# Stick-breaking attention: its cumulative sums in two fp32r passes, and its head pairs started beside other projections

## The chip, the cores and the metric

The kernel runs on one core of a Trainium2 chip. The metric is the device time of one execution in microseconds. The kernel before took 1529.96 us (median of three runs, 1529.09 to 1530.27).

## The reference, cut to what matters

Two network blocks of two layers each work on 256 tokens of width 1024. The change touches one mixer only, the stick-breaking attention of the second block's first layer:

```python
q, k, v = jnp.split(x @ w_in, 3, axis=-1)            # 16 heads of 64
for blk in range(S // Q_BLOCK):                      # two query blocks of 128
    z = einsum('bqhd,bkhd->bhqk', q[:, t0:L], k[:, :L]) * scale
    past = s_idx < t_idx
    log_fail = where(past, log_sigmoid(-z), 0.0)
    later = lax.cumsum(log_fail, axis=3, reverse=True) - log_fail
    a = where(past, exp(log_sigmoid(z) + later), 0.0)
    outs.append(einsum('bhqk,bkhd->bqhd', a, v[:, :L]))
return concatenate(outs) @ w_out
```

## The kernel before, in words

All matrix products with weights are done in three fp32r passes: a weight unit (128 x 1024 floats, 512 KB) is loaded by the SyncE queue into `w_raw`, ScalarE copies it to fp32r (`w_high`, L1493), VectorE subtracts (`w_low`, L1943), and TensorE multiplies high by high, high by low and low by high (L1092 to L1105). A planner (`Plan`) writes one list of steps, and every engine works through its own part of that list strictly in that order. Splits run five units ahead of the products (`prefetch`), and the split of a unit waits for the product of six units before it.

For the stick-breaking mixer (`stick_breaking`, L561) the input matrix of 3072 columns is cut into six panels of 512 columns and four units each: two of queries, two of keys (`sb_in`, features on the partitions, 24 products of 256 columns per unit), two of values (`sb_values`, tokens on the partitions, 12 products of 512 columns per unit). The 16 heads are worked on as 8 pairs. Keys stand on the partitions and queries along the row, so a head has a 128 x 384 tile: 256 queries against the first 128 keys, and the last 128 queries against the last 128 keys. A pair has 768 columns. Its steps:

- `sb_a`: TensorE makes the logits z in fp32 (L1317, L1319) in PSUM; ScalarE takes abs, exp and ln (L1717, L1719, L1721).
- `sb_b`: VectorE makes the fail term (L2278) and multiplies it by a mask of -1 and 0 over all 768 columns (L2280).
- `sb_c`: TensorE adds the sums over later keys onto z (L1332): per head, products of 256, 128 and 128 columns in fp32 with a triangular and an all-ones tile. VectorE clips and masks (L2287), ScalarE takes exp, the weights (L1728).
- `sb_d`: TensorE multiplies the weights by the values (L1345, L1347); ScalarE copies the high part (L1476), VectorE makes the low part (L1904) for the output product `sb_out`.

In iteration n of the loop stand `sb_d(n-3)`, `sb_c(n-2)`, `sb_b(n-1)`, then one or two weight units, then `sb_a(n)`. The units are the eight of `sb_values` (two in iterations 0 and 1, one in 2 to 5) and then four of `sb_out` (iterations 6 to 9). The copy of a finished value panel out of PSUM by ScalarE is `take_v` (L1704), the scaling of query and key panels by VectorE `take_qk` (L2266). The logits of even and odd pairs have slots 0 and 1 of PSUM (two banks each), the outputs of pairs banks 6 and 7 (slot 3). Panel 0 of `sb_out` gathers in slot 2, panel 1 in slot 1. After the loop the last four units of `sb_out` are done for the first 128 tokens and then for the others.

Of the kernel before, what the change touches and what calls it, by code (L numbers as in the profile page):

```python
# [14 lines left out]
P = 128  # L15
# [41 lines left out]
def weight_plan():  # L57
# [97 lines left out]
for _name, _w in (("ident", P), ("not_below", P), ("ones", P), ("cos_m", TT * ROPE // 2),  # L155
                  ("sin_m", TT * ROPE // 2), ("cos_g", TT * HD // 2), ("sin_g", TT * HD // 2),
                  ("inv_freq", DIL_ROT // 2), ("pool_edge", POOL_G * 2 * POOL_PAD), ("sb_neg", 3 * P),
                  ("sb_add", 3 * P), ("dil_add", 9 * P)):
    CONSTS[_name] = (_n, _n + _w)
    _n += _w  # L160
N_CONSTS = _n
N_HELD = CONSTS["sb_neg"][0]


def constants():
# [21 lines left out]
    past = np.concatenate([i[:, None] < np.arange(SEQ)[None, :], i[:, None] < i[None, :]], 1)  # L187
    put("sb_neg", np.where(past, -1.0, 0.0))
    put("sb_add", np.where(past, 0.0, MASKED))
# [18 lines left out]
def slot_of(name, layer, panel):  # L208
# [8 lines left out]
         "branch_gqa": (1, 0), "branch_pool": (2, 3), "branch_mla": (0, 1), "out": (0, 1),  # L217
         "ffn_up": (2, 1, 3, 2, 0, 1, 3, 2, 0, 1, 3, 2), "ffn_down": (0, 1), "sb_in": (0, 1, 2), "sb_values": (2,), "sb_out": (2, 1),
         "dil_qk": (1, 2, 0), "dil_values": (2,), "dil_out": (0, 2)}
# [6 lines left out]

BY_FEATURE = ("gates_early", "gates", "branch_gqa", "branch_pool", "branch_mla", "ffn_up", "sb_in", "ff_in")

# [18 lines left out]
class Plan:  # L247
# [313 lines left out]
    def stick_breaking(self):  # L561
        add, g, n_pairs = self.add, STAGE_SB, SB_H // 2
        add("load_sb")
        self.after(4, lambda: (add("diag", g), add("row", g)))
        self.whole("sb_in", 0, lambda panel: add("take_qk", panel))
        values = self.linear("sb_values", 0, lambda panel: add("take_v", panel))
        product = self.linear("sb_out", 0, None, SKEWED)
        add("sb_table")
        for n in range(n_pairs + 3):
# [14 lines left out]
        for _ in product:  # L584
            pass
# [130 lines left out]
class Kernel:  # L716
# [109 lines left out]
    def stick_memory(self):  # L826
        with ExitStack() as ctx:
# [4 lines left out]
            self.sb_masks = sb("sb_masks", 2 * NZ)  # L832
            part = lambda ap: ap.rearrange("p (j n) -> p j n", j=2)
            self.sb_weights = [part(sb(f"sb_weights{i}", 2 * NZ)) for i in range(2)]
            parts = [part(self.scr[:, i * 2 * NZ:(i + 1) * 2 * NZ]) for i in range(5)]
# [57 lines left out]
    def sync(self, eng):  # L893
# [5 lines left out]
        for step in self.plan.steps:  # L899
# [32 lines left out]
            elif kind == "load_sb":  # L932
                eng.dma_start(self.rows, dram["second_rows"][0, 0].partition_broadcast(P)
                              ).then_inc(sem("gains_loaded"), 16)
                at = CONSTS["sb_neg"][0]
                eng.dma_start(self.sb_masks, dram["consts"][:, at:at + 2 * NZ]).then_inc(sem("sb_masks_loaded"), 16)
# [29 lines left out]
    def operands(self, u):  # L966
# [18 lines left out]
        if name == "ffn_down":  # L985
            return self.ffn[l]
        if name in ("sb_in", "sb_values"):
            return self.features[STAGE_SB]
# [14 lines left out]
    def operand_ready(self, q, u, k, t):  # L1003
# [14 lines left out]
        elif name == "ffn_down":  # L1018
            q.wait_ge(sem("ffn_low"), at("ffn_split", l, k // 4))
        elif name in ("sb_in", "sb_values"):  # L1020
            q.wait_ge(sem("features_low"), at("turn", STAGE_SB, k // 2))
# [15 lines left out]
    def tensor(self, eng):  # L1037
        q = Queue(eng, None)
        sem, at, bank = self.sem, self.at, self.bank
        ident, ones, not_below = self.const("ident"), self.const("ones"), self.const("not_below")  # L1040

# [23 lines left out]
        for step in self.plan.steps:  # L1065
# [243 lines left out]
            elif kind == "sb_a":  # L1309
                j, = key  # L1310
                b = j % 2
                z = self.slot[b].rearrange("p (j n) -> p j n", j=2)
                q.wait_ge(sem("qk_taken"), at("take_qk", 3))
                acquire(2 * b, 2 * b + 1)
# [8 lines left out]
            elif kind == "sb_c":  # L1323
                j, = key
                b, fail = j % 2, self.sb_fail[j % 2]
# [113 lines left out]
    def taken_panel(self, step):  # L1439
# [10 lines left out]
        if kind == "take_qk":  # L1450
            return "sb_in", key[0]
        if kind == "take_v":
            return "sb_values", key[0]
        if kind == "take_dv":
# [8 lines left out]
    def scalar(self, eng):  # L1463
# [19 lines left out]
        for step in self.plan.steps:  # L1483
# [215 lines left out]
            elif kind == "take_v":  # L1699
                panel, = key  # L1700
                self.panel_done(q, "sb_values", 0, panel)
                a = by_token(self.acc("sb_values", panel))
                for t in range(TT):
# [3 lines left out]
            elif kind == "sb_table":  # L1707
                eng.preload_act_table_set("natural_log_exp_and_others")

            elif kind == "sb_a":  # L1710
# [9 lines left out]
                q.settle()  # L1720
                act(soft, soft, ACT.Ln, bias=1.0).then_inc(sem("soft_ready"), 1)  # L1721

            elif kind == "sb_c":
# [168 lines left out]
    def vector(self, eng):  # L1892
# [42 lines left out]
        for step in self.plan.steps:  # L1935
# [325 lines left out]
            elif kind == "take_qk":  # L2261
                panel, = key
                part = slice(4 * (panel % 2), 4 * (panel % 2) + 4)
                self.panel_done(q, "sb_in", 0, panel)
                q.wait_ge(sem("row_ready"), at("row", STAGE_SB))
                stt((self.sb_q if panel < 2 else self.sb_k)[:, part, :], by_tile(self.acc("sb_in", panel)),  # L2266
                    HD ** -0.5 if panel < 2 else 1.0, self.row(4), ALU.mult, ALU.mult).then_inc(sem("qk_taken"), 1)

            elif kind == "sb_b":
                j, = key  # L2270
                zs = self.slot[j % 2].rearrange("p (j n) -> p j n", j=2)[:, :, 0:NZ]
                neg = self.sb_masks[:, 0:NZ].rearrange("p (o n) -> p o n", o=1).to_broadcast([P, 2, NZ])
                fail = self.sb_fail[j % 2]
                q.wait_ge(sem("soft_ready"), at("sb_a", j))
                q.wait_ge(sem("sb_masks_loaded"), 16)
# [394 lines left out]
```

## Time and profile before

| what | us |
|---|---|
| median of three runs | 1529.96 |
| the profiled execution, its own time | 1527.88 |
| its span, first to last instruction | 1526.1 |
| TensorE busy in the span | 1493.5 |
| VectorE busy | 1045.5 |
| ScalarE busy | 839.8 |
| first logits of the mixer start | 870.98 |
| first pass of `sb_out` over the first tokens starts | 929.02 |

The span is told from the first to the last instruction; the profiled execution's own time is 1.8 us longer. A busy share is a mean over the whole span. In a timeline, a row that ends in `xN` merges N instructions of the same kind, and a bracket shows how long the engine stood idle before it and whose work released it. The start-to-start distance of two rows shows what an instruction costs in a stream; its own duration is longer, since instructions overlap.

### The profile page before, as it was taken

The numbers are of one execution on the slowest core, as the hardware profiler recorded it, in microseconds if no ns is written. First come the engines' busy times: TensorE is split into PE (matmuls) and PEld (weight loads), VectorE is DVE, ScalarE is ACT, GpSimd is POOL, SyncE is SP. The second block draws the span as 40 slices with busy tenths as digits, with TensorE's granted clock in tenths as the row PEclk, the third lists the DMA queues.
The fourth block names the chain that finished last, engine by engine and source line by source line (L and its number), as shares of the span: only waits on it lengthen the run. The fifth ranks groups of instructions, "written<-read, shape, count | busy, mean of one in ns | idle before, by whom it ended". The sixth has DMA issues, their size and how long they took to land. (4 is left out here: it accounts for less than half of the span.)

```text
span 1526.1 us, 23941 instructions
## 1 busy us (share of the span) xinstructions
PE 1493.5 (98%) x9872; PEld 1345.7 (88%) x9872; DVE 1045.5 (69%) x1549; ACT 839.8 (55%) x1243; POOL 58.3 (4%) x70
## 2 busy tenths in 40 slices
PE   7999999999999999999999999999999999999998
PEld 6999988998899989799989977998887888899886
DVE  6798677786578877687855567665466566766446
ACT  5565657555456555665644475554455555655434
POOL 1110000000021000000000000000010000100001
PEclk9999999999999999999999999999999999999999
DMA  7543455556555434556566523655646543555661
GB/s 245 178 150 111 141 176 166 171 192 196 188 172 167 128 109 151 180 176 197 168 198 211 166 97 111 217 177 196 194 161 208 165 128 125 169 170 185 201 193 69
DMA packets 73293, 255.75 MB, mean 168 GB/s; under 512 B 8416, under 2 KB 9568, under 8 KB 73184
## 3 DMA queue, kind: packets, MB, share of 16 engines
q1 hardware_dynamic: 72752, 253.78, 51.1%
q8 instruction: 78, 1.28, 0.3%
q10 hardware_dynamic: 432, 0.43, 0.1%
q14 instruction: 31, 0.25, 0.0%
HBM read 253.14 MB, written 1.05 MB: 167 GB/s over the span
## 5 line engine op out<-in xcount | busy, mean ns | idle before, releaser
L1943 DVE TENSOR_TENSOR w_low<-w_raw,w_high 128x1024 fp32r<-128x1024 f32 (+2 forms) x480 | 571.0, 1203 | 258.3 <-ACT w_high L1493 256.9
L1493 ACT ACTIVATE w_high<-w_raw 128x1024 fp32r<-128x1024 f32 (+2 forms) x480 | 495.1, 1042 | 314.3 <-PE psum L1105 174.0
L1092 PE MATMUL psum<-x_high,w_high 128*128 128x256 f32 x1504 | 429.9, 286 | 0.0
L1094 PE MATMUL psum<-x_low,w_high 128*128 128x256 f32 x1504 | 425.5, 283 | 0.0
L1095 PE MATMUL psum<-x_high,w_low 128*128 128x256 f32 x1504 | 425.5, 283 | 0.0
L1092 PEld LDWEIGHTS psum<-x_high,w_high 128*128 128x128 f32 x1504 | 288.4, 192 | 5.3 <-issue 4.6
L1094 PEld LDWEIGHTS psum<-x_low,w_high 128*128 128x128 f32 x1504 | 288.5, 192 | 0.4
L1095 PEld LDWEIGHTS psum<-x_high,w_low 128*128 128x128 f32 x1504 | 288.4, 192 | 0.0
L1101 PE MATMUL psum<-w_high,ff_high 128*128 128x512 f32 x256 | 100.0, 391 | 0.0
L1103 PE MATMUL psum<-w_low,ff_high 128*128 128x512 f32 x256 | 99.6, 389 | 0.0
L1105 PE MATMUL psum<-w_high,ff_low 128*128 128x512 f32 x256 | 99.6, 389 | 0.0
L1101 PE MATMUL psum<-w_high,x_high_next 128*128 128x512 f32 (+1 forms) x208 | 79.6, 383 | 3.7 <-DVE x_low_next L1956 2.3
L1101 PE MATMUL psum<-w_high,x_high 128*128 128x512 f32 (+2 forms) x208 | 79.3, 381 | 3.0 <-DVE w_low L1943 3.0
L1105 PE MATMUL psum<-w_high,x_low_next 128*128 128x512 f32 (+1 forms) x208 | 77.6, 373 | 0.0
L1103 PE MATMUL psum<-w_low,x_high_next 128*128 128x512 f32 (+1 forms) x208 | 77.6, 373 | 0.0
L1105 PE MATMUL psum<-w_high,x_low 128*128 128x512 f32 (+2 forms) x208 | 77.1, 371 | 0.0
L1103 PE MATMUL psum<-w_low,x_high 128*128 128x512 f32 (+2 forms) x208 | 77.0, 370 | 0.0
L1101 PE MATMUL psum<-w_high,ffn_high 128*128 128x512 f32 x176 | 68.7, 390 | 0.0
L1103 PE MATMUL psum<-w_low,ffn_high 128*128 128x512 f32 x176 | 68.5, 389 | 0.0
L1105 PE MATMUL psum<-w_high,ffn_low 128*128 128x512 f32 x176 | 68.5, 389 | 0.0
L1092 PE MATMUL psum<-x_high_next,w_high 128*128 128x256 f32 x224 | 63.5, 284 | 0.0
L1095 PE MATMUL psum<-x_high_next,w_low 128*128 128x256 f32 x224 | 63.4, 283 | 0.0
(264 smaller groups left out, 2396.6 us busy)
## 6 DMA issues: line engine op xcount, KB each, us to landing
w_raw<-in_weights SPq DMA_DIRECT2D x450, 512.0 KB, 4.1
w_raw<-in_weights SPq DMA_DIRECT2D x16, 384.0 KB, 3.0
w_raw<-in_weights SPq DMA_DIRECT2D x8, 416.0 KB, 5.5
rows<-in_second_rows SPq DMA_DIRECT2D x4, 512.0 KB, 4.9
w_raw<-in_weights SPq DMA_DIRECT2D x6, 256.0 KB, 2.8
residual<-in_x SPq DMA_DIRECT2D x2, 512.0 KB, 5.9
out<-residual SPq DMA_DIRECT2D x2, 512.0 KB, 2.7
dil_masks<-in_consts SPq DMA_DIRECT2D x1, 576.0 KB, 5.7
```

Source lines behind the costliest of these rows:

```text
L1092: eng.matmul(o, wh[:, j, cut], high[:, k, :], start=k == 0 and f % 2 == 0, stop=False, skip_group_check=True)
L1094: eng.matmul(o, wh[:, j, cut], low[:, k, :], start=False, stop=False, skip_group_check=True)
L1095: d = eng.matmul(o, wl[:, j, cut], high[:, k, :], start=False, stop=end, skip_group_check=True)
L1101: eng.matmul(o, high[:, k, cut], wh[:, j, :], start=k == 0, stop=False, skip_group_check=True)
L1103: eng.matmul(o, high[:, k, cut], wl[:, j, :], start=False, stop=False, skip_group_check=True)
L1105: d = eng.matmul(o, low[:, k, cut], wh[:, j, :], start=False, stop=end, skip_group_check=True)
L1493: act(self.unit_view(self.wh, u), raw, ACT.Copy).then_inc(sem("w_high"), 1)
L1943: tt(self.unit_view(self.wl, u), raw, self.unit_view(self.wh, u), ALU.subtract).then_inc(sem("w_low"), 1)
```

## The change

The sums of `sb_c` become fp32r: the fail term is split into a high and a low part (ScalarE copies, VectorE subtracts), and per head and part there are two products, one of 384 columns with the triangle and one of 128 columns with the ones. The sign moves from the mask into the two constant tiles, which ScalarE writes as fp32r once (`sb_ones`). The mask in `sb_b` is applied to the two diagonal blocks of 128 columns alone.

The first half of the queries and of the keys is projected before the loop; the second half of the queries, the first values, the second half of the keys and the second values are projected in the loop, in this order, with 2, 3, 4, 3, 2, 1 and 1 units in iterations 0 to 6. `sb_out` follows with one unit in each of iterations 7 to 10. Pairs 0 to 3 need the first halves only.

```diff
-            plan += [("sb_in", 0, "w_in_sb_2", D, panels_of(0, 2 * D)),
-                     ("sb_values", 0, "w_in_sb_2", D, panels_of(2 * D, 3 * D)),
+            plan += [(name, 0, "w_in_sb_2", D, [(c, c + PANEL) for c in at])
+                     for name, at in (("sb_in", (0, D)), ("sb_late_q", (PANEL,)), ("sb_values", (2 * D,)),
+                                      ("sb_late_k", (D + PANEL,)), ("sb_late_v", (2 * D + PANEL,)))]
...
-"sb_in": (0, 1, 2), "sb_values": (2,), "sb_out": (2, 1),
+"sb_in": (0, 1), "sb_late_q": (2,),
+         "sb_values": (3,), "sb_late_k": (2,), "sb_late_v": (2,), "sb_out": (2, 1),
...
-        self.whole("sb_in", 0, lambda panel: add("take_qk", panel))
-        values = self.linear("sb_values", 0, lambda panel: add("take_v", panel))
+        self.whole("sb_in", 0, lambda panel: add("take_qk", 2 * panel))
+        def beside():
+            yield from self.linear("sb_late_q", 0, lambda panel: add("take_qk", 1))
+            yield from self.linear("sb_values", 0, lambda panel: add("take_v", 0))
+            yield from self.linear("sb_late_k", 0, lambda panel: add("take_qk", 3))
+            yield from self.linear("sb_late_v", 0, lambda panel: add("take_v", 1))
+        others = beside()
...
-            if n < 6:
-                for _ in range(2 if n < 2 else 1):
-                    next(values)
-            elif n < 10:
+            if n < 7:
+                for _ in range((2, 3, 4, 3, 2, 1, 1)[n]):
+                    next(others)
+            else:
                 next(product)
...
# TensorE, sb_a
-                q.wait_ge(sem("qk_taken"), at("take_qk", 3))
+                q.wait_ge(sem("qk_taken"), at("take_qk", 2 if j < 4 else 3))
# TensorE, sb_c
-                q.wait_ge(sem("fail_ready"), at("sb_b", j))
+                q.wait_ge(sem("sb_ones_ready"), 1)
+                q.wait_ge(sem("fail_low"), at("sb_b", j))
                 for i in range(2):
-                    for o, m, r in ((z[:, i, 0:SEQ], not_below, fail[:, i, 0:SEQ]),
-                                    (z[:, i, P:SEQ], ones, fail[:, i, SEQ:NZ]),
-                                    (z[:, i, SEQ:NZ], not_below, fail[:, i, SEQ:NZ])):
-                        d = eng.matmul(o, m, r, start=False, stop=True, skip_group_check=True)
+                    for fail in self.sb_parts[j % 2]:
+                        eng.matmul(z[:, i, 0:NZ], below, fail[:, i, 0:NZ], start=False, stop=True, skip_group_check=True)
+                        d = eng.matmul(z[:, i, P:SEQ], every, fail[:, i, SEQ:NZ], start=False, stop=True,
+                                       skip_group_check=True)
...
# ScalarE
             elif kind == "sb_table":
                 eng.preload_act_table_set("natural_log_exp_and_others")
+                act(self.sb_ones[:, 0:P], self.const("not_below"), ACT.Copy, scale=-1.0)
+                act(self.sb_ones[:, P:2 * P], self.const("ones"), ACT.Copy, scale=-1.0).then_inc(sem("sb_ones_ready"), 1)
...
+            elif kind == "sb_b":
+                q.wait_ge(sem("fail_ready"), at(*step))
+                if j >= 2:
+                    q.wait_ge(sem("later_summed"), at("sb_c", j - 2))
+                split_high(self.sb_parts[j % 2][0], self.sb_fail[j % 2], "fail_high")
...
# VectorE, sb_b
-                tt(fail, fail, neg, ALU.mult).then_inc(sem("fail_ready"), 1)
+                q.step(tt(fail[:, :, 0:P], fail[:, :, 0:P], past, ALU.mult))
+                tt(fail[:, :, SEQ:NZ], fail[:, :, SEQ:NZ], past, ALU.mult).then_inc(sem("fail_ready"), 1)
+                high, low = self.sb_parts[j % 2]
+                q.wait_ge(sem("fail_high"), at(*step))
+                q.settle()
+                tt(low, fail, high, ALU.subtract).then_inc(sem("fail_low"), 1)
```

## Rows read from the trace of the kernel before

**Rows 1.** The page, part 1: busy time, share of the span and instructions of each engine.

```profile
PE 1493.5 (98%) x9872; PEld 1345.7 (88%) x9872; DVE 1045.5 (69%) x1549; ACT 839.8 (55%) x1243; POOL 58.3 (4%) x70
```

**Rows 2.** Timeline of TensorE, one iteration of the loop: start, duration, what.

```profile
889.45 0.71 PE L1317 MATMUL psum<-sb_q,sb_k 64*128 64x256 f32 x4
...
890.31 0.66 PE L1345 MATMUL psum<-sb_weights,sb_v 128*64 128x256 f32 x4
...
891.11 2.02 PE L1332 MATMUL psum<-scratch,consts 128*128 128x256 f32 x12
892.89 0.48 PE L1101 MATMUL psum<-w_high,x_high 128*128 128x512 f32 x1
...
895.50 0.39 PE L1105 MATMUL psum<-w_high,x_low 128*128 128x512 f32 x1
895.82 0.71 PE L1317 MATMUL psum<-sb_q,sb_k 64*128 64x256 f32 x4
```

**Rows 3.** Timeline of ScalarE in the loop: start, duration, what, idle before it.

```profile
890.43 0.81 ACT L1717 ACTIVATE scratch<-psum 128x768 f32<-128x768 f32 x1 [0.39 <-PE psum L1319]
...
892.90 0.37 ACT L1476 ACTIVATE sb_out_high<-psum 128x256 fp32r<-128x256 f32 x1
894.62 0.85 ACT L1728 ACTIVATE sb_weights<-scratch 128x768 f32<-128x768 f32 x1 [1.35 <-DVE scratch L2287]
895.37 1.04 ACT L1493 ACTIVATE w_high<-w_raw 128x1024 fp32r<-128x1024 f32 x1
...
902.69 1.25 ACT L1704 ACTIVATE sb_v<-psum,stat 128x512 f32<-128x512 f32 x2
903.83 0.81 ACT L1717 ACTIVATE scratch<-psum 128x768 f32<-128x768 f32 x1
...
909.72 0.79 ACT L1717 ACTIVATE scratch<-psum 128x768 f32<-128x768 f32 x1
```

**Rows 4.** Timeline of VectorE in the same iteration.

```profile
893.30 0.42 DVE L1904 SCALAR_TENSOR_TENSOR sb_out_low<-psum,sb_out_high 128x256 fp32r<-128x256 f32 x1 [2.00 <-ACT sb_out_high L1476]
893.64 0.95 DVE L2287 SCALAR_TENSOR_TENSOR scratch<-psum,sb_masks 128x768 f32<-128x768 f32 x1
894.50 0.95 DVE L2278 SCALAR_TENSOR_TENSOR scratch<-psum,scratch 128x768 f32<-128x768 f32 x1
895.49 0.96 DVE L2280 TENSOR_TENSOR scratch<-scratch,sb_masks 128x768 f32<-128x768 f32 x1
```

**Rows 5.** Timeline of TensorE in the dilated mixer: fp32r products of 384 columns, and transposes.

```profile
1230.24 0.34 PE L1101 MATMUL psum<-w_high,x_high_next 128*128 128x384 f32 x1
1230.42 0.35 PE L1103 MATMUL psum<-w_low,x_high_next 128*128 128x384 f32 x1
...
1232.52 1.06 PE L1050 MATMUL psum<-consts,dil_tokens 128*128 128x128 f32 x8 [0.53 <-DVE dil_q L1900]
1233.34 0.43 PE L1101 MATMUL psum<-w_high,x_high_next 128*128 128x384 f32 x1
```

**Rows 6.** Groups by line and shape, whole span: busy us, mean ns, idle before.

```profile
L1925 DVE TENSOR_TENSOR scratch<-mla_tokens,rope_tables 128x256 f32<-128x256 f32 x16 | 5.7, 419 | 0.1
L1943 DVE TENSOR_TENSOR w_low<-w_raw,w_high 128x768 fp32r<-128x768 f32 x16 | 15.3, 956 | 12.8 <-ACT w_high L1493 12.8
L1493 ACT ACTIVATE w_high<-w_raw 128x768 fp32r<-128x768 f32 x16 | 13.2, 840 | 6.6 <-PE psum L1105 6.6
```

**Rows 7.** Timeline of TensorE at the end of the loop.

```profile
925.28 0.47 PE L1101 MATMUL psum<-w_high,sb_out_high 128*128 128x512 f32 x1 [1.14 <-DVE scratch L2287]
...
929.60 0.40 PE L1105 MATMUL psum<-w_high,sb_out_low 128*128 128x512 f32 x1
930.04 0.51 PE L1101 MATMUL psum<-w_high,sb_out_high 128*128 128x512 f32 x1
```

**Rows 8.** The last product, and a stretch behind it: length, engines' busy time, PEclk, DMA share, GB/s.

```profile
1519.01 0.39 PE L1105 MATMUL psum<-w_high,x_low_next 128*128 128x512 f32 x1
...
1522.00:1522.50 0.50, 0.00 (x0) 0.00 (x0) 0.47 (x2) 0.00 (x0) 0.00 (x0) 0.91 0.00 0
```

More of the change, by code:

```diff
@@ L156 @@
                   ("sin_m", TT * ROPE // 2), ("cos_g", TT * HD // 2), ("sin_g", TT * HD // 2),
-                  ("inv_freq", DIL_ROT // 2), ("pool_edge", POOL_G * 2 * POOL_PAD), ("sb_neg", 3 * P),
+                  ("inv_freq", DIL_ROT // 2), ("pool_edge", POOL_G * 2 * POOL_PAD), ("sb_past", 3 * P),
                   ("sb_add", 3 * P), ("dil_add", 9 * P)):
@@ L161 @@
 N_CONSTS = _n
-N_HELD = CONSTS["sb_neg"][0]
+N_HELD = CONSTS["sb_past"][0]
 def constants():
@@ L187, in constants @@
     past = np.concatenate([i[:, None] < np.arange(SEQ)[None, :], i[:, None] < i[None, :]], 1)
-    put("sb_neg", np.where(past, -1.0, 0.0))
+    put("sb_past", np.where(past, 1.0, 0.0))
     put("sb_add", np.where(past, 0.0, MASKED))
@@ L225 @@
 TURNED = {"ffn_up": (0, 0), "ff_in": (2, 0)}
-BY_FEATURE = ("gates_early", "gates", "branch_gqa", "branch_pool", "branch_mla", "ffn_up", "sb_in", "ff_in")
+BY_FEATURE = ("gates_early", "gates", "branch_gqa", "branch_pool", "branch_mla", "ffn_up", "sb_in", "sb_late_q", "sb_late_k", "ff_in")
+SB_LINEARS = ("sb_in", "sb_late_q", "sb_values", "sb_late_k", "sb_late_v")
 DIL_BANKS = (3, 6, 3)
@@ L583, in stick_breaking @@
                 add("sb_a", n)
-        for _ in product:
+        for _ in (*others, *product):
             pass
@@ L833, in stick_memory @@
             part = lambda ap: ap.rearrange("p (j n) -> p j n", j=2)
+            self.sb_parts = [[part(sb(f"sb_fail_{name}{i}", 2 * NZ, F32R)) for name in ("high", "low")] for i in range(2)]
+            self.sb_ones = sb("sb_ones", 2 * P, F32R)
             self.sb_weights = [part(sb(f"sb_weights{i}", 2 * NZ)) for i in range(2)]
@@ L934, in sync @@
                               ).then_inc(sem("gains_loaded"), 16)
-                at = CONSTS["sb_neg"][0]
+                at = CONSTS["sb_past"][0]
                 eng.dma_start(self.sb_masks, dram["consts"][:, at:at + 2 * NZ]).then_inc(sem("sb_masks_loaded"), 16)
@@ L986, in operands @@
             return self.ffn[l]
-        if name in ("sb_in", "sb_values"):
+        if name in SB_LINEARS:
             return self.features[STAGE_SB]
@@ L1019, in operand_ready @@
             q.wait_ge(sem("ffn_low"), at("ffn_split", l, k // 4))
-        elif name in ("sb_in", "sb_values"):
+        elif name in SB_LINEARS:
             q.wait_ge(sem("features_low"), at("turn", STAGE_SB, k // 2))
@@ L1039, in tensor @@
         sem, at, bank = self.sem, self.at, self.bank
-        ident, ones, not_below = self.const("ident"), self.const("ones"), self.const("not_below")
+        ident, ones = self.const("ident"), self.const("ones")
         free = {}
@@ L1324, in tensor @@
                 j, = key
-                b, fail = j % 2, self.sb_fail[j % 2]
+                b, below, every = j % 2, self.sb_ones[:, 0:P], self.sb_ones[:, P:2 * P]
                 z = self.slot[b].rearrange("p (j n) -> p j n", j=2)
-                q.wait_ge(sem("fail_ready"), at("sb_b", j))
+                q.wait_ge(sem("sb_ones_ready"), 1)
+                q.wait_ge(sem("fail_low"), at("sb_b", j))
                 for i in range(2):
-                    for o, m, r in ((z[:, i, 0:SEQ], not_below, fail[:, i, 0:SEQ]),
-                                    (z[:, i, P:SEQ], ones, fail[:, i, SEQ:NZ]),
-                                    (z[:, i, SEQ:NZ], not_below, fail[:, i, SEQ:NZ])):
-                        d = eng.matmul(o, m, r, start=False, stop=True, skip_group_check=True)
+                    for fail in self.sb_parts[j % 2]:
+                        eng.matmul(z[:, i, 0:NZ], below, fail[:, i, 0:NZ], start=False, stop=True, skip_group_check=True)
+                        d = eng.matmul(z[:, i, P:SEQ], every, fail[:, i, SEQ:NZ], start=False, stop=True,
+                                       skip_group_check=True)
                 d.then_inc(sem("later_summed"), 1)
@@ L1450, in taken_panel @@
         if kind == "take_qk":
-            return "sb_in", key[0]
+            return (("sb_in", 0), ("sb_late_q", 0), ("sb_in", 1), ("sb_late_k", 0))[key[0]]
         if kind == "take_v":
-            return "sb_values", key[0]
+            return ("sb_values", "sb_late_v")[key[0]], 0
         if kind == "take_dv":
@@ L1700, in scalar @@
                 panel, = key
-                self.panel_done(q, "sb_values", 0, panel)
-                a = by_token(self.acc("sb_values", panel))
+                name, p = self.taken_panel(step)
+                self.panel_done(q, name, 0, p)
+                a = by_token(self.acc(name, p))
                 for t in range(TT):
@@ L1721, in scalar @@
                 act(soft, soft, ACT.Ln, bias=1.0).then_inc(sem("soft_ready"), 1)
+            elif kind == "sb_b":
+                j, = key
+                q.wait_ge(sem("fail_ready"), at(*step))
+                if j >= 2:
+                    q.wait_ge(sem("later_summed"), at("sb_c", j - 2))
+                split_high(self.sb_parts[j % 2][0], self.sb_fail[j % 2], "fail_high")
             elif kind == "sb_c":
@@ L2263, in vector @@
                 part = slice(4 * (panel % 2), 4 * (panel % 2) + 4)
-                self.panel_done(q, "sb_in", 0, panel)
+                name, p = self.taken_panel(step)
+                self.panel_done(q, name, 0, p)
                 q.wait_ge(sem("row_ready"), at("row", STAGE_SB))
-                stt((self.sb_q if panel < 2 else self.sb_k)[:, part, :], by_tile(self.acc("sb_in", panel)),
+                stt((self.sb_q if panel < 2 else self.sb_k)[:, part, :], by_tile(self.acc(name, p)),
                     HD ** -0.5 if panel < 2 else 1.0, self.row(4), ALU.mult, ALU.mult).then_inc(sem("qk_taken"), 1)
@@ L2271, in vector @@
                 zs = self.slot[j % 2].rearrange("p (j n) -> p j n", j=2)[:, :, 0:NZ]
-                neg = self.sb_masks[:, 0:NZ].rearrange("p (o n) -> p o n", o=1).to_broadcast([P, 2, NZ])
                 fail = self.sb_fail[j % 2]
+                past = self.sb_masks[:, 0:P].rearrange("p (o n) -> p o n", o=1).to_broadcast([P, 2, P])
                 q.wait_ge(sem("soft_ready"), at("sb_a", j))
```

3 lines of the change are left out of this document (2 added, 1 removed).

## The prediction

> **What bounds the kernel now.** I read the page's busy shares first: TensorE is busy 98% of the span, VectorE 69%, ScalarE 55% [rows 1]. So a change pays only where TensorE gets less to do, or where it stops waiting. The shares are means over stages, so I then read the three queues of the stick-breaking loop, which is all that the change touches. One iteration there takes 6.37 us on TensorE without a gap [rows 2]: logits of a pair (889.45 to 890.31, 0.86), weighted values (to 891.11, 0.80; I use 0.81), sums (to 892.89, 1.78), one unit of weight products (to 895.82, 2.93). In the unit, products of 512 columns follow each other by 0.23, and 0.32 passes where fp32 and fp32r products meet (895.50 to 895.82): an edge costs 0.09.
>
> ScalarE and VectorE look idle there by their shares, but they hand one pair back and forth. I name the steps: A (abs, exp, ln of pair n), H (high part of an output), W (exp of the weights), S (split of a unit). ScalarE starts A at 890.43, H 2.47 later, W at 894.62, S 0.75 after W, and the next A after only 0.39 us of waiting for TensorE [rows 3]. Where a 1.14 us copy of values delayed it, it ran from A (903.83) to A (909.72) without waiting: 5.89 us is the chain's own cycle, so S to A is 5.89 - 2.47 - 1.72 - 0.75 = 0.95. The chain has 0.5 us of slack below TensorE's 6.37, and this is the number on which everything rests. VectorE's links: low part of the output 0.40 after H, the logit step 0.34 later, the fail step 0.86 later, the masking product 0.99 later [rows 4].
>
> **What the change removes.** Sums: six fp32 products per pair (1.78 us) become four of 384 and four of 128 columns in fp32r. A 384-column fp32r product takes 0.18 (1230.24 to 1230.42); eight 128-column transposes with their weight loads take 0.82 including one edge, 0.09 each [rows 5]. 4 x (0.18 + 0.09) = 1.08 us, 0.70 less per pair, 5.6 us over eight. No row shows a 128-column fp32r product. From below: 0.06, the 384 price by columns; from above: 0.22, the fp32 price (1.78 over eight 128-column shares). I take the transposes' 0.09 as nearest; sums lie between 0.96 and 1.60. The Trainium skill (TensorE: Matmul & The Clock Gate, LDWEIGHTS) gives about 107 ns to load 128 weight columns, which would set the small product: sums 1.15, some 0.3 us more at the end; the transposes' 0.09 speaks for slightly less.
>
> Masks: one 768-element masking product (0.96 us) becomes two of 256 elements; such a product takes 0.42 [rows 6], the second starts 0.33 behind the first, so the last ends 0.75 after the first begins.
>
> Order: half of the query, key and value panels move into the loop, so 20 units instead of 12 lie beside the pairs, in portions 2, 3, 4, 3, 2, 1, 1, 1, 1, 1, 1. Units are conserved: the move alone is worth nothing except for waits. It removes two. The unit at 925.28 waited 1.14 us, since it writes the banks of the last pair's logits before they are read; it now comes behind the last weighted values. And the last output's low part, which made the first pass wait (929.60 to 930.04 instead of 0.23: 0.21), is done before [rows 7]. Loads: the same weights in the same number of DMAs; splits run five units ahead, which hides them. Two copies for the ones tile at the table load stand ahead of the loop, where ScalarE waits for TensorE: nothing, and at most 0.8 if that cover were gone. New panel reuse of one slot waits for a 1.2 us take behind 2.7 us of other products: nothing.
>
> **What it adds.** The sums' input must be split: ScalarE copies 768 elements to fp32r (0.84) and VectorE subtracts (0.96) [rows 6]. The costly thing is where this stands. ScalarE's copy F waits for VectorE's masking, and behind F in ScalarE's queue stand S and the next A. F starts 0.75 + 0.03 = 0.78 after the first mask; 0.03 is the hop between the two engines (the logit step, 893.64 and 0.95 long, ends at 894.59, W starts at 894.62). ScalarE's cycle is now A to H 2.47, low 0.40, logit step 0.34, fail step 0.86, mask 0.99, F 0.78, S 0.75, A 0.95: 7.54 us, plus 0.95 per further unit. TensorE's cycle with one unit is 0.86 + 0.81 + 1.17 (sums with the edge that they take over) + 2.83 = 5.67. So the early iterations, with 2 to 4 units (8.4 to 14 us of TensorE), hide the chain, and those with one unit do not. After A starts, the low part reaches TensorE 2.47 + 0.40 + 0.34 + 0.86 + 0.99 + 0.78 + 0.87 + 0.96 + 0.1 = 7.77 later; the logit step frees its banks after 4.27; W is ready after 5.14 (0.1 for a hop to TensorE is my estimate).
>
> The times from the start of logits(4) on TensorE, where the hiding ends: logits(3) started at -8.41, A(3) at -7.42, so A(4) starts at -7.42 + 8.49 = 1.07, A(5) at 8.61. Iteration 6 has the last value unit, and its take (1.14 of ScalarE, 902.69 to 903.83 in [rows 3]) stands between S and A(6): A(6) at 17.29, A(7) at 24.83. TensorE: values(2) 0.86, sums(3) 1.67, unit to 5.67, logits(5), values(3) to 7.34; sums(4) need 8.84: waits 1.50. Unit to 12.84, logits(6) 12.88: 0.04. Values(4) need the taken second half of the value panel, at 16.15 + 1.25 + 0.1 = 17.50, TensorE is there at 13.74: waits 3.76. Sums(5), unit, logits(7), values(5) to 23.98; sums(6) need 25.06: 1.08. Unit to 29.06; values(6) need W(6) at 29.97: 0.91; sums(7) come at 30.78 and need 32.60: 1.82. From there nothing is late. Waits together 9.11 us.
>
> Sum: 9.1 - 5.6 - 1.14 - 0.21 = +2.2 us. The profiled execution took 1527.88, so 1530.1; it lies 2.1 below the median of the runs, 1529.96, which gives **1532.2**. Since the chain decides the end, a cheaper or dearer sum shows only in about four pairs (the first three and the last): at 0.96 the result is 1531.7, at 1.60 it is 1534.3. An error of 0.15 in a link of the chain counts four times, 0.6 us.
>
> **Rivals.** (1) The clock falls. Behind the last product (1519.01, 0.39 long) the granted clock goes to its lower level in the half microsecond from 1522.00, where it reads 0.91, that is at about 1522.4, 3.0 us after the work stopped [rows 8]. My wait ahead of values(4) is 3.76, the longest in the loop. Against it: the wait is barely longer than that one sample, and it shrinks if the take is sooner. At 1.2 GHz values(4) and sums(5) take 2.0 us more, of which 1.2 reaches the chain; if the unit behind is slow as well, A(7) is 3.3 late. So +1.2 to +3.3, 1534.5 in the middle. The same page of the Trainium skill (HAM oscillation) says that idle gaps between bursts of products send the array back to half clock; by that rule this rival comes about, and its price is the one above.
>
> (2) TensorE stays the bound. If the fp32r copy, the masks and the order cost the chain nothing, the whole 5.6 + 1.14 + 0.21 = 6.9 us is won: 1523.1. This is the case that ends faster. It decides at a chain cycle of 5.67 us. For it speaks only that both engines have free time by their shares; against it that the old chain, without F, already cycled at 5.89 with nothing to wait for [rows 3].
>
> (3) The sums of 128 columns cost as much as in fp32: 1534.3, as above. Against it, the products of 256 to 512 columns show no such price.
>
> (4) The waits overlap better than in my table (masks cheaper, a take ahead of its place): half of 9.1 goes, 1527.7 to 1529.
>
> **How the numbers follow.** Forecast 52%, clock 20%, TensorE-bound 10%, small products dear 6%, waits smaller 12%. What a measurement of this kernel can tell from no change is 0.2%, 3.1 us: below 1526.9 or above 1533.0. The forecast, with some 1.3 us of spread from prices and chain links, puts a third of its chance above 1533.0: 16 of 52. Slower: 16 + 20 + 6 = 42%. Faster: 10% and a little of case 4: 12%. Same: 46%. The likeliest case's own range is 1530.4 to 1534.2; the range reaches down into case 4 and up over the clock case: 1527.5 to 1536.0.
>
> **What would show it.** In the changed kernel's TensorE queue the sums of a pair take about 1.1 us (over 1.5: rival 3). ScalarE's start of A to the next A is about 7.5 us in the iterations with one unit, with ScalarE waiting for the mask before F. TensorE waits in the last five iterations, over 8 us in all, the longest ahead of values(4) and released by the value copy; no waits before logits(4). The last product unit no longer waits for the logit step. Clock at 1.00 throughout refutes rival 1. TensorE without waits in the loop would make the forecast wrong, as would an A to A cycle under 6 us.

## The result, and the profile after

The changed kernel took 1532.46 us (median of 11 runs, 1531.67 to 1534.48); the kernel before, beside it on the same chip, 1528.46 (11 runs, 1527.29 to 1530.92). The ratio is 1.0025, 95% interval 1.0016 to 1.0034: slower, by 0.25%. A second series gave 1.0021 (1.0012 to 1.0030). (The ratio is estimated from all runs of a series; it need not be the quotient of the two medians.) On the forecast's own scale, where slower began at 1533.0, 1532.46 counts as no change; but measured side by side the change is slower, and the interval is clear of 1. The forecast of 1532.2 lies 0.3 from the median, but that is luck in part: it was +2.2 us on a base of 1529.96, and the kernel before, run more often, stood at 1528.46. By the medians the change cost 4.0 us in this series and 2.4 in the second. So there are two questions: whether the forecast's terms were right, and where the up to 1.8 us come from that it lacks.

The page, part 1, of the changed kernel (columns as in [rows 1]):

```profile
PE 1492.3 (98%) x9840; PEld 1345.1 (88%) x9840; DVE 1050.9 (69%) x1565; ACT 845.7 (55%) x1253; POOL 58.3 (4%) x70
```

TensorE is busy 1.2 us less, although its sums are cheaper by 4.6 us (8 x 0.58, below), so other products took longer; and the span grew from 1526.1 to 1530.5, so there are waits. TensorE in one iteration of the loop (answers to [rows 2]):

```profile
893.37 0.45 PE L1346 MATMUL psum<-sb_fail_high,sb_ones 128*128 128x384 f32 x1
893.65 0.22 PE L1347 MATMUL psum<-sb_fail_high,sb_ones 128*128 128x128 f32 x1
893.71 0.39 PE L1346 MATMUL psum<-sb_fail_low,sb_ones 128*128 128x384 f32 x1
893.94 0.22 PE L1347 MATMUL psum<-sb_fail_low,sb_ones 128*128 128x128 f32 x1
...
894.57 0.44 PE L1116 MATMUL psum<-w_high,x_high 128*128 128x512 f32 x1
...
897.48 0.71 PE L1332 MATMUL psum<-sb_q,sb_k 64*128 64x256 f32 x4
```

The sums of a pair take 893.37 to 894.57, 1.20 us with one edge; the forecast had 1.17 with the edge, the old sums took 1.78. Rival 3 (1.60) is out. The two prices inside are not those of the forecast: a 128-column product takes 0.06, and the 384-column product ahead of it 0.23 instead of 0.18. Only their sum, 0.29 against 0.27, came out. And the edge is not all in the sums: the first product of the unit behind them takes 0.28 instead of 0.23 as well. From the sums to the next logits 4.11 us pass (893.37 to 897.48), where the forecast had 4.00 (1.17 + 2.83) and the kernel before 4.71 [rows 2]; the whole iteration, from logits at 891.70, takes 5.78 against 5.67 and 6.37. So a pair saves 0.59 us, and eight save 4.7, not 5.6.

ScalarE in the loop (answers to [rows 3]):

```profile
892.71 0.79 ACT L1737 ACTIVATE scratch<-psum 128x768 f32<-128x768 f32 x1
...
895.16 0.36 ACT L1492 ACTIVATE sb_out_high<-psum 128x256 fp32r<-128x256 f32 x1
896.88 0.85 ACT L1755 ACTIVATE sb_weights<-scratch 128x768 f32<-128x768 f32 x1 [1.35 <-DVE scratch L2321]
898.53 0.84 ACT L1492 ACTIVATE sb_fail_high<-scratch 128x768 fp32r<-128x768 f32 x1 [0.81 <-DVE scratch L2310]
899.28 1.04 ACT L1509 ACTIVATE w_high<-w_raw 128x1024 fp32r<-128x1024 f32 x1
900.23 0.79 ACT L1737 ACTIVATE scratch<-psum 128x768 f32<-128x768 f32 x1
...
907.76 1.25 ACT L1721 ACTIVATE sb_v<-psum,stat 128x512 f32<-128x512 f32 x2
908.90 0.81 ACT L1737 ACTIVATE scratch<-psum 128x768 f32<-128x768 f32 x1
```

A to A is 7.52 us (892.71 to 900.23; forecast 7.54), and 8.67 with the value copy in it (8.68). The copy F (898.53) stands behind the weights, idle for 0.81 until VectorE's second mask is done, and in front of the split and of the next A: where the forecast put it. VectorE there (answers to [rows 4]):

```profile
896.76 0.95 DVE L2307 SCALAR_TENSOR_TENSOR scratch<-psum,scratch 128x768 f32<-128x768 f32 x1
897.74 0.43 DVE L2309 TENSOR_TENSOR scratch<-scratch,sb_masks 128x256 f32<-128x256 f32 x1
898.08 0.42 DVE L2310 TENSOR_TENSOR scratch<-scratch,sb_masks 128x256 f32<-128x256 f32 x1
899.41 0.96 DVE L2314 TENSOR_TENSOR sb_fail_low<-scratch,sb_fail_high 128x768 fp32r<-128x768 f32 x1 [0.91 <-ACT sb_fail_high L1492]
```

All of TensorE's waits from the first one-unit iteration to the end of the mixer (forecast: 1.50, 3.76, 1.08, 0.91, 1.82), and its wait at the entry of the dilated mixer:

```profile
900.42 0.44 PE L1346 MATMUL psum<-sb_fail_high,sb_ones 128*128 128x384 f32 x1 [1.21 <-DVE sb_fail_low L2314]
909.06 0.66 PE L1361 MATMUL psum<-sb_weights,sb_v 128*64 128x256 f32 x4 [3.62 <-ACT sb_v L1721]
921.85 0.66 PE L1361 MATMUL psum<-sb_weights,sb_v 128*64 128x256 f32 x4 [0.50 <-ACT sb_weights L1755]
924.50 0.44 PE L1346 MATMUL psum<-sb_fail_high,sb_ones 128*128 128x384 f32 x1 [1.77 <-DVE sb_fail_low L2314]
...
1168.03 0.47 PE L1116 MATMUL psum<-w_high,x_high_next 128*128 128x512 f32 x1 [2.28 <-DVE x_low_next L1983]
```

The unit behind the loop and the first pass no longer wait [rows 7]. In stretches, with the granted clock as the number after POOL's:

```profile
908.00:909.50 1.50, 0.44 (x4) 0.36 (x6) 1.11 (x1) 1.50 (x3) 0.00 (x0) 1.00 0.00 0
909.50:909.80 0.30, 0.30 (x7) 0.15 (x2) 0.00 (x0) 0.27 (x2) 0.00 (x0) 0.77 0.00 0
909.80:913.00 3.20, 3.20 (x14) 2.90 (x11) 0.99 (x2) 1.90 (x3) 0.00 (x0) 0.50 0.52 164
913.00:913.50 0.50, 0.50 (x3) 0.38 (x3) 0.50 (x2) 0.07 (x1) 0.00 (x0) 0.92 0.00 0
1169.00:1170.00 1.00, 1.00 (x4) 0.77 (x3) 0.00 (x0) 0.97 (x1) 0.75 (x2) 0.54 1.02 418
1170.00:1172.00 2.00, 2.00 (x7) 1.52 (x6) 1.23 (x1) 0.00 (x0) 0.00 (x0) 0.50 0.78 317
1172.00:1174.00 2.00, 2.00 (x9) 1.64 (x8) 0.21 (x1) 1.06 (x1) 0.00 (x0) 0.88 0.83 254
```

Behind the 3.62 wait TensorE goes to 1.2 GHz from about 909.7 to 913: the fall of rival 1 has come true (its price has not, see below). It does so a second time in the dilated mixer, 250 us later, behind the 2.28 wait. The profiled execution of before has that same wait, at 1165.31, and stays at 1.00 behind it (timeline, then a stretch):

```profile
1165.31 0.47 PE L1101 MATMUL psum<-w_high,x_high_next 128*128 128x512 f32 x1 [2.28 <-DVE x_low_next L1956]
```

```profile
1167.00:1169.00 2.00, 2.00 (x10) 1.67 (x9) 1.23 (x1) 0.79 (x2) 0.12 (x1) 1.00 0.91 373
```

The profiled executions are 4.40 us apart (1527.88 and 1532.28). From the stick-breaking mixer's first row sums to the transposes behind it they take 108.72 (830.31 to 939.03) and 110.99 (830.84 to 941.83): +2.27 in the mixer, the forecast's +2.2, with one fall of the clock in it. From there to the end it is +1.6: the wait at the dilated entry ends 226.3 and 226.2 behind the mixer, so these 1.6 lie behind that wait, where the second fall is. The start of the mixer is 0.5 later, before anything that the change touches.

### The profile page after: what moved, and what is told of

Its sections match the earlier page's. It is cut to its first block and busy times, and to the rows that moved or that the text cites. A ratio compares the mean times of both kernels' runs of the same rounds, so it can differ in the third digit from the quotient of the medians.

```text
span 1530.5 us, 23918 instructions
## 1 busy us (share of the span) xinstructions
PE 1492.3 (98%) x9840; PEld 1345.1 (88%) x9840; DVE 1050.9 (69%) x1565; ACT 845.7 (55%) x1253; POOL 58.3 (4%) x70
```

## The experiments

**The changed kernel once more** (no edit).

> The changed kernel as it is, once more beside the kernel before. Chain theory (ScalarE's copy of the fail term lengthens the hand-over between ScalarE and VectorE): 4.0 us slower than before as measured first, of which the mixer gives about 2, with the wait ahead of values(4) near 3.6 us and the clock falling in it. Clock theory: the rest (about 1.6 us) comes from the clock falling a second time, behind the 2.3 us wait at the entry of the dilated mixer; if so this profile, should the clock stay up there, shows a span nearer 1529 than 1530.5.

1532.26 us (11 runs), before 1529.87 (25 runs), ratio 1.0021 (1.0012 to 1.0030). That it is slower stands. The distance is 2.4 here and 4.0 in the first series, because the median of before moves. The executions of before lie in two groups, 1527.3 to 1528.4 at a mean granted clock of 0.999 (8 of 25) and 1529.3 to 1530.3 at 0.998 (16 of 25), and one is at 1531.5 with 0.996. The changed kernel's lie at 1530.5 and 1530.6 (0.998), 1531.9 to 1532.7 (0.997 or 0.996) and 1534.1 to 1534.5 (0.995). So the number of falls differs from execution to execution. The profile of this run shows three. One is at the start of the program, ahead of this mixer, behind a TensorE wait of 2.18 that all the kernels have in about that length (the profile of before waits 2.38 there and stays at 1.00); the other two are in the mixer (0.72 and 0.58):

```profile
36.00:40.00 4.00, 2.83 (x13) 2.83 (x14) 3.91 (x6) 1.68 (x5) 0.06 (x1) 0.63 0.51 144
...
912.00:916.00 4.00, 4.00 (x19) 3.44 (x16) 1.82 (x3) 1.86 (x4) 0.00 (x0) 0.72 0.34 124
...
928.00:932.00 4.00, 4.00 (x12) 3.14 (x12) 2.15 (x3) 1.79 (x2) 0.00 (x0) 0.58 0.42 131
```

The last follows a wait of 1.78 ahead of the last sums; behind the same wait (1.77) the first profile stayed at 1.00. At the dilated entry the clock stays up in this profile. Its span is all the same 1532.7 and not near 1529, as the expectation had it, since the falls are elsewhere: the one ahead of the mixer makes it start 1.8 later (832.60 against 830.84), and the mixer takes 112.99, 2.0 more than in the first profile.

**The fp32r copy on VectorE.** The other half of the theory: F's place in ScalarE's queue is what costs.

```diff
-            elif kind == "sb_b":                       # ScalarE
-                split_high(self.sb_parts[j % 2][0], self.sb_fail[j % 2], "fail_high")
...
+                q.step(ts(high, fail, 1.0, None, ALU.mult))   # VectorE, in place of the wait
+                q.settle()
                 tt(low, fail, high, ALU.subtract).then_inc(sem("fail_low"), 1)
```

> The fp32r copy of the fail term is done by VectorE, right behind the masks, instead of ScalarE. Chain theory: ScalarE's cycle from A to A returns to 5.9, VectorE's becomes 6.06 us; waits ahead of sums(4), values(4), sums(6), sums(7) shrink to about 1.5, 0.6, 1.2, 1.2 and the end of the loop comes 4.6 us sooner than in the changed kernel: 1527.8, some 1 to 2.5 us under the kernel before. Rival (the waits come from VectorE's work, or from the order of the units): moving work onto VectorE makes it slower than the changed kernel, 1533 or more.

1525.20 us (9 runs), ratio to before 0.9976 (0.9967 to 0.9986), 7 us under the changed kernel: moving one copy per pair turns the change from a loss into a gain. ScalarE's A starts at 891.65 and 897.54, 5.89 apart, to the hundredth the cycle of before. It came out 2.6 below what I expected. Of this 0.8 lies in the mixer (5.4 us shorter instead of 4.6; VectorE's copy takes 0.56, ScalarE's took 0.84), and the rest goes with falls: neither of the first profile's two is in this one, and six of the nine executions are at a mean clock of 0.999, which none of the changed kernel's 22 reached.

```profile
891.65 0.81 ACT L1737 ACTIVATE scratch<-psum 128x768 f32<-128x768 f32 x1 [1.54 <-PE psum L1334]
...
897.54 0.79 ACT L1737 ACTIVATE scratch<-psum 128x768 f32<-128x768 f32 x1
```

```profile
897.05 0.42 DVE L2303 TENSOR_TENSOR scratch<-scratch,sb_masks 128x256 f32<-128x256 f32 x1
897.50 0.56 DVE L2306 TENSOR_SCALAR sb_fail_high<-scratch 128x768 fp32r<-128x768 f32 x1
898.10 0.96 DVE L2308 TENSOR_TENSOR sb_fail_low<-scratch,sb_fail_high 128x768 fp32r<-128x768 f32 x1
```

The waits that are left are 0.93, 0.57, 0.67 and 1.07, 3.2 us in all; the mixer takes 105.58.

**Each half alone: the sums in the old order, and the order with the old sums.** In the first the units stay as before (two panels of queries and keys ahead of the loop, one unit in most iterations), and the sums, the masks and F are those of the change. The second is the reverse.

```diff
# sums_old_order keeps, order_only takes:
-            for _ in range(2 if n < 2 else 1): next(values)
+            for _ in range((2, 3, 4, 3, 2, 1, 1)[n]): next(others)
```

> The fp32r sums and the masks alone, in the old order of the units (one unit beside each pair from iteration 2 on). Chain theory: the cycle of 7.54 us now governs iterations 2 to 8, where TensorE needed 6.37; the loop ends some 8 us later than before: 1536.5 (1535 to 1538). Rival (TensorE's shorter sums carry through): 0.6 us less per pair, 1523.7.

> The new order of the units with the old fp32 sums and the old mask. Chain theory: the 5.9 us cycle stays under TensorE's 6.37; a wait of about 1.0 us ahead of values(4) for the late value panel, minus the 1.14 and 0.21 us of removed waits: -0.35, that is 1528.1, no change. Rival (the order is what costs): 3 to 4 us slower, as the whole change.

The sums alone: 1542.23 us (5 runs), ratio 1.0076 (1.0062 to 1.0090), 12 us slower than before and 5.7 more than expected. The order alone: 1528.86 (11 runs), ratio 0.9997 (0.9988 to 1.0006), no change, with one wait of 0.87 left in the loop and a mixer 0.9 us shorter. Waits of the sums in the old order, and the clock around two of them:

```profile
886.29 0.44 PE L1333 MATMUL psum<-sb_fail_high,sb_ones 128*128 128x384 f32 x1 [1.39 <-DVE sb_fail_low L2299]
893.82 0.44 PE L1333 MATMUL psum<-sb_fail_high,sb_ones 128*128 128x384 f32 x1 [1.70 <-DVE sb_fail_low L2299]
908.88 0.44 PE L1333 MATMUL psum<-sb_fail_high,sb_ones 128*128 128x384 f32 x1 [1.68 <-DVE sb_fail_low L2299]
...
917.56 0.44 PE L1333 MATMUL psum<-sb_fail_high,sb_ones 128*128 128x384 f32 x1 [1.77 <-DVE sb_fail_low L2299]
```

```profile
892.00:900.00 8.00, 6.30 (x27) 5.02 (x26) 5.09 (x7) 5.76 (x8) 0.00 (x0) 0.79 0.21 68
900.00:912.00 12.00, 10.21 (x67) 8.04 (x66) 7.26 (x9) 9.70 (x14) 0.00 (x0) 1.00 0.19 62
...
916.00:924.00 8.00, 6.44 (x28) 5.22 (x28) 5.09 (x7) 5.76 (x9) 0.00 (x0) 0.79 0.22 66
```

Five waits for the low part, 8.3 us, at the cycle of 7.53 (886.29 to 893.82). Behind 1.70 and the first 1.77 the clock falls, behind 1.39, 1.68 and a second 1.77 it does not. The mean clock of the median executions is 0.993, of the quickest (1537.6) 0.997: so the excess over my estimate, which had the waits alone, goes with falls; the quickest, with the two falls shown, lies 1.1 above the estimate. The two halves are not additive (+12.4 and about 0 against +2.4 to +4.0 together): the order's worth is that iterations with 2 to 4 units hide the longer chain. That the order alone brings no gain in the median although its mixer is shorter goes with the clock again: none of its 11 executions is at 0.999, and its profile shows a fall at the dilated entry.

**Filling the waits.** To part the wait from the clock I put products that write an unused bank into the waits. They compute nothing that is used.

```diff
+        def fill(b, n):
+            acquire(b)
+            for _ in range(n):
+                eng.matmul(bank[b], self.features[0][0][:, 0, 0:P], self.features[0][0][:, 2:4, :], start=True, stop=True,
+                           skip_group_check=True)
...
+                if j == 4:                        # ahead of values(4): after_fill, after_fill_all
+                    fill(b, 14)
...
+                if j in (4, 6, 7):                # ahead of sums(j): after_fill_all
+                    fill(6 + (j == 7), {4: 4, 6: 3, 7: 6}[j])
...
+                if (g, j) == (STAGE_DIL, 3):      # the dilated entry: before_fill and both of the others
+                    fill(7, 8)
```

> The kernel before, with eight products of 512 columns into an unused bank in TensorE's 2.3 us wait at the entry of the dilated mixer (they feed nothing). Clock theory (executions of one kernel stand about 2 us apart by how often the clock falls in TensorE's waits): nearly all executions at a mean clock of 0.999 and near 1527.8, few at 0.998 and 1530. Rival (the two groups of times have another cause): the same two groups as the kernel before.

> The changed kernel with the same eight products there, and fourteen in the wait ahead of values(4), where TensorE stands 3.6 us. Clock theory: no fall at either place, 1529.7 to 1530.3, that is 1.9 to 2.5 above before_fill: what the waits themselves cost without the clock. A fall may remain behind the 1.8 us wait for sums(7). Rival (the clock adds nothing that counts): 1532.3, as the changed kernel.

> after_fill with further products that feed nothing in the waits ahead of sums(4), sums(6) and sums(7) (4, 3 and 6 of 512 columns). Clock theory: no fall is left in the mixer, so all executions stand at 0.999 or above and within 1529.8 to 1530.8; this is the cost of the waits alone, 2.2 us over before_fill at no fall. Rival (another cause of the 2 us groups): executions at 1532 and above remain as in after_fill.

Kernel before with the one fill: 1528.14 us (11 runs), before in the same series 1529.83 (30 runs), ratio 0.9994 (0.9985 to 1.0002). In a median that is not shown to be faster, but the mean clock is 0.999 in 9 of 11 executions, where it is 0.999 in 12 of 30 without the fill; the groups at 0.999 and below are 2 us apart. The wait shrinks from 2.28 to 0.45. This speaks for the dilated entry, which the change does not touch, as the place where most falls of the kernel before happen, and for these falls as the reason that its median moves from series to series. The one profile of the kernel before shows no fall there; but of all the profiled executions here, nine stand 2.28 at this place and four of them show the fall behind it, and of the four with the fill none does. The executions that are left below 0.999 may be those with the fall at the start of the program, which no fill covers: a fall at 36 to 41 us is in four of the thirteen profiles.

The changed kernel with two fills: 1531.04 (11 runs), ratio 1.0014 (1.0005 to 1.0023), above the expected 1529.7 to 1530.3. Five executions are at 0.999 or 1.000 (1529.83 to 1530.67), six at 0.998 or 0.997 (1531.04 to 1533.66). Its profile shows one fall, behind the 1.77 wait ahead of sums(7), and there it costs 1.5 us: the mixer takes 112.19, and 110.67 with all the waits filled. With fills in all the waits (on another chip, beside its own before): 1530.45 (11 runs, ten of them 1529.71 to 1530.6), ratio 1.0008 (0.9999 to 1.0017) to a before of 1529.73 (21 runs). That run's mean clock is 0.999 or more in ten of eleven, so it is to be put beside those executions of before that are at 0.999 too: ten, 1527.68 to 1528.55, middle 1528.05. The difference is 2.4 us. This is what the change costs without falls, next to the forecast's +2.2. Its mixer takes 110.67, with a granted clock of 1.00 from 896 to 944.

**Other orders of the steps.** First the changed kernel with `sb_c(n-2)` ahead of `sb_d(n-3)`, so that the sums reach ScalarE's weights sooner; then the same with the copy on VectorE.

```diff
+            if 2 <= n < n_pairs + 2:
+                add("sb_c", n - 2)
             if n >= 3:
                 add("sb_d", n - 3)
-            if 2 <= n < n_pairs + 2:
-                add("sb_c", n - 2)
```

> The changed kernel with sb_c(n-2) ahead of sb_d(n-3) in each iteration. Chain theory: the logit step and the exp of the weights no longer stand behind the high and low part of an output; ScalarE's cycle from A to A drops from 7.52 to about 6.07 us, the fail term's low part is ready 6.3 us behind A instead of 7.8, and values(4) find their panel taken. The loop ends 5.4 us sooner: about 1527. Rival (the copy of the value panel alone is the cost): only the 3.6 us wait shrinks, and sums arrive later since values stood ahead of them: 1530 or more.

> Both edits, the fp32r copy on VectorE and sb_c ahead of sb_d. Chain theory: the low part is ready 6.0 us behind A, waits of 0.5 to 0.7 us ahead of three sums and none ahead of values(4); 2.6 us under dve_high: 1522.6. Rival (dve_high is bound by TensorE already): 1525.

Both expectations fell, and so did the rivals' mechanisms, though the first rival's 1530 or more holds as a number. In the first kernel no wait ahead of values(4) is left, but ScalarE's A to A is 7.42 (894.77 to 902.19) where I expected 6.07, and the sums wait 1.75, 2.55 and 0.66. The first took 1534.27 us (8 runs), ratio 1.0027 (1.0017 to 1.0038); the second 1532.73 (10 runs), ratio 1.0022 (1.0013 to 1.0031), 10 over what I expected and 7.5 over the same copy in the old order. The three engines in the second, in the order of time:

```profile
902.22 0.44 PE L1346 MATMUL psum<-sb_fail_high,sb_ones 128*128 128x384 f32 x1 [1.47 <-DVE sb_fail_low L2308]
...
903.62 0.96 DVE L2315 SCALAR_TENSOR_TENSOR scratch<-psum,sb_masks 128x768 f32<-128x768 f32 x1 [0.32 <-PE psum L1347]
904.62 0.85 ACT L1748 ACTIVATE sb_weights<-scratch 128x768 f32<-128x768 f32 x1 [1.24 <-DVE scratch L2315]
905.37 0.36 ACT L1492 ACTIVATE sb_out_high<-psum 128x256 fp32r<-128x256 f32 x1
905.77 0.43 DVE L1924 SCALAR_TENSOR_TENSOR sb_out_low<-psum,sb_out_high 128x256 fp32r<-128x256 f32 x1 [1.18 <-ACT sb_out_high L1492]
...
906.11 0.95 DVE L2300 SCALAR_TENSOR_TENSOR scratch<-psum,scratch 128x768 f32<-128x768 f32 x1
909.49 0.44 PE L1346 MATMUL psum<-sb_fail_high,sb_ones 128*128 128x384 f32 x1 [1.29 <-DVE sb_fail_low L2308]
```

The swap puts the output's high part behind the weights in ScalarE's queue, and its low part ahead of the fail term in VectorE's. VectorE, which has finished the logit step at 904.58, waits 1.18 for a copy that itself waits for the weights. Now the sums are in a loop of their own: sums, logit step, weights, high part, low part, fail term, masks, copy, low part, sums, and it takes 7.27 (902.22 to 909.49) where TensorE has 5.7 of work. I had counted the step that gets earlier, and not the one that gets into the loop.

So the output went behind both, with the copy on VectorE (on that other chip too): `sb_c(n-2)`, `sb_b(n-1)`, `sb_d(n-3)`.

> dve_high with the order sb_c(n-2), sb_b(n-1), sb_d(n-3) in each iteration: values come behind the sums on TensorE, and the split of the output behind the fail term on VectorE. Loop theory from dve_high_swap (7.27 us from sums to sums, because the logit step, exp, high and low part of an output all stand between one sums and the next fail term): without the two output steps the loop is 1.4 + 0.86 + 0.98 + 0.35 + 0.45 + 0.59 + 0.96 + 0.1 = 5.7 us, about TensorE's own; waits under 0.8 us, none ahead of values(4); 2 us under dve_high: 1523.2. Rival (TensorE must not do sums ahead of values): 1530 or more, as dve_high_swap.

> dve_high_late_out with the eight products in the wait at the entry of the dilated mixer, as in before_fill. Clock theory: fewer executions with a fall, median 0.5 to 1 us lower: 1522.5, nearly all at 0.999. Rival: no difference to dve_high_late_out.

1525.87 us (10 runs), ratio 0.9981 (0.9972 to 0.9991), not shown to be better than the plain VectorE copy (0.9976, 0.9967 to 0.9986), where I expected 2 us less. The waits in the loop fell from 3.2 us to two, of 0.40 and 0.56, and the mixer from 105.58 to 104.39. What the mixer won goes with the clock: none of its ten executions is at 0.999, where six of nine were, and its profile shows a fall at the dilated entry. With the entry filled, 1524.18 (6 runs), ratio 0.9968 (0.9956 to 0.9979): the lowest median, 5.5 us under before, but its interval overlaps that of the plain VectorE copy, and the kernel before beside it has no fill. In the medians the fill took 1.7 us off this kernel, more than the 0.5 to 1 expected (four of the six are below all ten without it). But the median lies 1.7 above the expected 1522.5, and three of six executions are at 0.999, not nearly all; its profile (0.998) has the fall at the start of the program. The fall at the entry, without the fill:

```profile
1160.00:1163.00 3.00, 1.40 (x6) 1.21 (x7) 2.23 (x7) 1.72 (x5) 0.59 (x1) 1.00 1.01 415
1163.00:1166.50 3.50, 3.50 (x10) 2.72 (x10) 1.23 (x1) 0.71 (x2) 0.33 (x2) 0.51 0.83 297
1166.50:1168.00 1.50, 1.50 (x8) 1.24 (x7) 0.69 (x1) 0.78 (x1) 0.00 (x0) 1.00 0.56 221
```

## Why the prediction came out as it did

**The bound.** Right. ScalarE's cycle was read as 5.89 in the trace of before [rows 3] and is 5.89 again as soon as F is off its queue; with F it is 7.52 against a forecast of 7.54. Rival 2, TensorE as the bound, fell.

**What the change removes.** Sums 1.20 against 1.17, nearly right as a total and wrong in its parts (0.23 + 0.06, not 0.18 + 0.09). The 5.6 us over eight pairs were too much: TensorE's iteration came to 5.78, not 5.67, so it is 4.7. The waits of 1.14 and 0.21 [rows 7] are gone.

**What it adds.** Waits of 7.10 us against 9.11: 1.21, 3.62, 0.50 and 1.77 match four terms within 0.41, and the wait of sums(6) for 1.08 is missing. The traces say where it went: at 1.2 GHz TensorE was late enough that its own lateness covered it, which is why the mixer still comes out at +2.27. With the fall filled away, the sums(6) wait is back, 0.94 in the run with two fills, and the mixer with all fills takes 110.67 against 110.99: inside the mixer the fall behind values(4) costs only 0.3, the rest of it lies beside waits. Without a fall the mixer is thus 1.95 us longer than before (110.67 against 108.72). The forecast's +2.2 is that close because two errors cancel: its waits are some 0.9 too long (9.11, where those measured without a fall, 1.21, 3.62, 0.94, 0.69 and 1.77, make 8.2), and its saving on TensorE is 0.9 too large. Rival 4, which would have halved the waits, fell; rival 3 fell with sums of 1.20.

**The clock.** This is the step that failed, in chance, in size and in place. The forecast gave the fall behind values(4) 20%, because 3.76 was barely longer than the 3.0 seen behind the last product [rows 8]. Both profiles of the changed kernel show it, but there it cost 0.3 us, not 1.2 to 3.3. And there are falls behind shorter waits, of 1.70, 1.77, 1.78 and 2.28, which the forecast did not consider; behind the wait ahead of sums(7), with which the loop ends, a fall cost 1.5 us, and 2.0 in the second profile. The 3.0 was the time the clock held on after work had stopped for good; it was no bound for a wait with work behind it, where the fall comes after TensorE has resumed (909.06, fall at about 909.7). And I priced one fall in the changed mixer, while the base has a fall of its own in more than half its executions (46 of 76 are below 0.999), as the fill speaks for mostly at a place that the change doesn't touch. Where no wait absorbs it, one more fall costs about 2 us in this kernel: in the last series the groups of before are 1528.05 and 1530.1 in the middle. The rule of the Trainium skill (TensorE: Matmul & The Clock Gate, HAM oscillation) that idle gaps between bursts of products send the array back to half clock agrees with these rows. The section speaks of longer gaps than the 1.70 to 2.28 us here, and the measurements decide. That a gap of the same length does so in one execution and not in another, these runs show besides.

**Shown and not shown.** Shown: the chain through F costs the change its gain (moving F alone wins 7 us, 5.4 of them in the mixer), and without falls the change is +2.4. Shown: falls happen behind the waits, and with the waits filled ten of eleven executions of the changed kernel are at 0.999 or more, where none of 22 was. Not settled in full: how much of the 4.0 against the forecast's 2.2 is falls added by the change and how much is the base at a quiet moment. Most of it looks like the base: the changed kernel stood at 1532.46 and 1532.26 in its two series, while before moved from 1528.46 to 1529.73 and more (up to 1529.87), close to the 1529.96 that the forecast started from. Nor is it known why one 2.28 us wait leads to a fall and its twin does not.

## What to carry to other kernels

When a busy engine gets its work cut, follow the helper engines' queues through one iteration, in order, and add up the whole cycle with every instruction that stands behind a wait: one copy of 0.84 us in ScalarE's queue cost this change 7 us, 5.4 in the mixer and the rest with falls of the clock, and putting it on the engine that made its input won them back. Before an order is changed, list what the swap puts between two links of that cycle, not only what it brings forward. TensorE waits of 1.7 us and more were followed by a fall of the clock in some executions here, at 0.3 to 2 us each, so look at the mean clock of each execution before calling 2 us between medians a gain.

## What the runs showed of the hardware

- Behind a 128-column fp32r product with its own weights the next product follows in 0.06 us, but the 384-column one ahead of it takes 0.23 (0.18 in a stream of its own kind, [rows 5]). These are distances from start to start.
- A copy of 768 fp32 elements to fp32r takes 0.56 us on VectorE and 0.84 on ScalarE; the subtraction of the same size, with two tensors read, takes 0.96. The Trainium skill (VectorE: DVE Perf Modes, the perf-mode tier table) gives one-source operations between fp32 tensors in SBUF a double rate that two-source ones don't get in fp32; the trace agrees, 0.56 against 0.96.
- At a granted clock of 0.50 products of 512 columns follow each other by 0.43 instead of 0.23 us (changed kernel, 1170 to 1172).
- A fall of the clock costs what the waits behind it don't cover: 0.3 us inside the loop, where the helper engines' chain decides, 1.5 to 2 us behind the last sums and at the dilated entry.
